# Sample attention and mLSTM in one block: heads between the key and value steps, a zeroed score bank, the sample rows of x read a second time

## The chip, the core and the metric

The kernel runs on one core of a Trainium2 chip. The metric is the device time of one execution in microseconds (us), median of several runs. A core has engines with a queue of instructions each: TensorE (PE; its weight loads are listed as PEld), VectorE (DVE), ScalarE (ACT), and SyncE (SP), which here issues most transfers. An engine takes its instructions in order and waits at semaphores. Matmul results go to the accumulator memory PSUM, which the kernel uses in banks of 512 columns.

## What is computed

One step of a decoder layer for a prompt of 256 tokens and for 8 samples of 4 tokens (32 rows). A normalised input goes through one projection that feeds two branches, an mLSTM with a matrix memory and a windowed attention; both are projected, gated and added, and a mixture of 32 experts follows. The change touches the two branches. From the reference, cut:

```python
# attention of a sample, per group (window, dilation): keys gathered from the cache and the new tokens
kg, vg = kf[:, idx], vf[:, idx]
s = einsum('bthe,btjhe->bthj', q, kg) * (E ** -0.5)
p, l, lse = masked_softmax_stats(s, valid)
o = einsum('bthj,btjhe->bthe', p, vg) / l[..., None]
...
# mLSTM, per chunk and head
b = cumsum(fc);  dmat = where(causal, b_j - b_s + ic_s, -inf);  mj = maximum(b + m, max(dmat))
sc  = (q k^T) * exp(dmat - mj);   a_int = exp(b + m - mj)
num = sc @ v + a_int * (C q);     den = sum(sc) + a_int * (n q)
h   = num / maximum(abs(den), exp(-mj))
C_new = a_c * C + sum_s ws_s v_s k_s^T;   n_new = a_c * n + sum_s ws_s k_s
...
h = h * sigmoid(o);  h = h * rsqrt(mean(h*h) + EPS) * norm_w        # per head
u = sigmoid(ga) * (hA @ w_pa) + sigmoid(gb) * (hB @ w_pb)
```

## The kernel before

The program is a row of blocks; all engines meet at the end of a block. The blocks are: the input projection, the prompt's attention, **the sample attention** (block at line 748), **the mLSTM** (block at line 957), the projection of both branches with the router (line 1309), the experts (line 1853) and the end. The order inside a block is written out by hand, one function for each engine.

*Sample attention.* The keys and values of the caches come in 16 loads of 1792 KB (KT_cache, then VK, line 757) through four slots KV: kv0, kv1 and two parts of za. Load i waits until step i-4 has been used (s_used). TensorE transposes the new queries and keys, makes the new scores, and takes eight key steps (line 777), which sum masked queries (qmask, which VectorE makes) times keys in psA. VectorE masks the scores and takes their maximum (lines 885 and 889), ScalarE takes exp (814), VectorE normalises (892), TensorE transposes the probabilities (784), ScalarE copies them out (818), and eight value steps follow (794). Then VectorE picks out each row's own sample (own, hBs), and TensorE turns the result for hBT. Beside the key steps VectorE also does the mLSTM's gate arithmetic on rows of 4 partitions: lf, prefix sums and maxima by doubling, and six pieces of xrow (877, 880).

*mLSTM.* Columns of cg, emj and ws are made from the rows by small products (1001 to 1005) and copied to colsb. For each of the four heads of the prompt: transposed q and k (994, copied out by ScalarE at 1095 and VectorE at 1141), scores (1013, 1015) with the row maxima (1017), exponent arguments (1152 to 1154), exp (1100), weights wt (1159), the state product (1026, 1029) of keys weighted by VectorE (wk, 1145), which ScalarE copies out for C_p and n_p, and the output products (1034 to 1036), which VectorE divides and gates (finish, 1132 to 1135). The next head's transposes are issued ahead of a head's state product. After the heads come the samples: scores, weights, and the products on eight state tiles of 1 MB (CT, 1070), which SP loads from the block's start into parts of za, xT, h and a tile of its own. As tiles in za are used, w_pa is loaded over them in four pieces (973). VectorE normalises the heads, and the transposed result hAT (1063, 1079, 1207, 1220) feeds the next block, whose first product is line 1298.

## Time and profile before

| | |
|---|---|
| median of 3 runs | 1636.36 us (1634.91 to 1640.58) |
| the profiled execution | 1636.94 us |
| its span, first to last instruction | 1635.2 us |
| mean granted TensorE clock | 0.965 |
| TensorE, VectorE, ScalarE busy | 1488.8, 650.2, 216.8 us |
| transfers | 584.17 MB, 357 GB/s over the span |
| sample attention, first product to the next block's | 365.53 to 445.35 us |
| mLSTM, likewise | 445.35 to 511.90 us |

The profile is of one execution, and its times count from the span's start. An engine's busy time is that in which it executes an instruction; waits are not counted. "PEclk" is the granted share of TensorE's full clock, 1.00 for 2.4 GHz and 0.50 for 1.2 GHz. "DMA share" is the mean busy share of the core's 16 transfer engines. An fp32 matmul leaves two records, so "x24" are twelve matmuls. In a list in order of time the brackets at a row's end give the engine's idle time before it and what released it.

### The profile page before, as it was taken

The numbers are of one execution on the slowest core, as the hardware profiler recorded it, in microseconds if no ns is written. First come the engines' busy times: TensorE is split into PE (matmuls) and PEld (weight loads), VectorE is DVE, ScalarE is ACT, GpSimd is POOL, SyncE is SP. The second block draws the span as 40 slices with busy tenths as digits, with TensorE's granted clock in tenths as the row PEclk, the third lists the DMA queues.
The fourth block names the chain that finished last, engine by engine and source line by source line (L and its number), as shares of the span: only waits on it lengthen the run. The fifth ranks groups of instructions, "written<-read, shape, count | busy, mean of one in ns | idle before, by whom it ended". The sixth has DMA issues, their size and how long they took to land. (4 is left out here: it accounts for less than half of the span.)

```text
span 1635.2 us, 20121 instructions
## 1 busy us (share of the span) xinstructions
PE 1488.8 (91%) x8061; PEld 710.5 (43%) x8061; DVE 650.2 (40%) x1050; ACT 216.8 (13%) x390; POOL 0.3 (0%) x5
## 2 busy tenths in 40 slices
PE   6999999864686998999999999999999999999977
PEld 4777776651553444333333333333333333333333
DVE  5555565345043614233333324333333333323343
ACT  2101110221030002011111101111011111101122
POOL 0000000000000000000000000000000000000000
PEclk9999999987787998999999999999999999999988
DMA  5888889499667992899999999999999999999960
GB/s 185 312 333 312 308 324 365 185 311 426 258 221 273 378 408 103 338 396 428 428 429 428 428 429 428 429 429 428 428 428 429 429 428 427 429 429 429 428 254 29
DMA packets 70528, 584.17 MB, mean 357 GB/s; under 512 B 6060, under 2 KB 8592, under 8 KB 42704
## 3 DMA queue, kind: packets, MB, share of 16 engines
q1 hardware_dynamic: 63856, 572.07, 85.7%
q10 hardware_dynamic: 6624, 11.41, 1.9%
q8 instruction: 37, 0.61, 0.1%
q14 instruction: 11, 0.09, 0.0%
HBM read 569.78 MB, written 67.80 MB: 390 GB/s over the span
## 5 line engine op out<-in xcount | busy, mean ns | idle before, releaser
L1676 PE MATMUL eG<-ring,hBT 128*64 128x512 f32 x1008 | 262.6, 599 | 2.3 <-DMA ring<-w 2.3
L1676 PE MATMUL eL<-ring,hBT 128*64 128x512 f32 x1008 | 259.0, 592 | 0.0
L1718 PE MATMUL eY<-ring,hBT 128*64 128x512 f32 x1024 | 233.9, 598 | 22.0 <-ACT hBT L1758 22.0
L1827 DVE SCALAR_TENSOR_TENSOR h<-eS,rgg,h 128x512 f32<-128x512 f32 (+1 forms) x192 | 135.0, 743 | 208.9 <-PE eS L1702 205.1
L1800 DVE TENSOR_SCALAR xT<-eG 128x512 f32<-128x512 f32 x32 | 22.1, 692 | 301.9 <-PE eL L1676 301.9
L411 PE MATMUL psT<-whi,xhi 128*128 128x512 f32 x336 | 136.6, 407 | 2.8 <-ACT zg L485 2.8
L1676 PEld LDWEIGHTS eL<-ring,hBT 128*64 128x64 f32 x1008 | 72.4, 137 | 143.9 <-issue 143.9
L411 PE MATMUL psT<-wlo,xhi 128*128 128x512 f32 x336 | 132.2, 393 | 0.0
L411 PE MATMUL psT<-whi,xlo 128*128 128x512 f32 x336 | 131.5, 391 | 0.0
L1718 PEld LDWEIGHTS eY<-ring,hBT 128*64 128x64 f32 x1024 | 68.0, 136 | 144.5 <-issue 114.9
L1676 PEld LDWEIGHTS eG<-ring,hBT 128*64 128x64 f32 x1008 | 66.1, 136 | 129.5 <-issue 120.1
L352 DVE CAST whi<-wraw 128x2048 fp32r<-128x2048 f32 x41 | 50.3, 1228 | 121.6 <-PE psT L415 121.4
L353 DVE TENSOR_TENSOR wlo<-wraw,whi 128x2048 fp32r<-128x2048 f32 x42 | 96.3, 2292 | 1.4
L1652 PE MATMUL eA<-zg,selU 128*64 128x512 f32 x396 | 92.3, 602 | 1.7 <-DVE selU L1789 1.7
L1767 ACT ACTIVATE xT<-xT 128x512 f32<-128x512 f32 x32 | 20.2, 631 | 467.6 <-DVE xT L1800 467.6
L411 PEld LDWEIGHTS psT<-whi,xhi 128*128 128x128 f32 x336 | 63.4, 189 | 29.0 <-issue 16.4
L1702 PE MATMUL eS<-yS,selT 128*128 128x512 f32 x192 | 71.8, 455 | 3.4 <-DVE yS L1813 2.7
L411 PEld LDWEIGHTS psT<-whi,xlo 128*128 128x128 f32 x336 | 63.4, 189 | 14.1
L411 PEld LDWEIGHTS psT<-wlo,xhi 128*128 128x128 f32 x336 | 63.5, 189 | 11.9
L1298 PE MATMUL pX<-za,xT 128*128 128x512 f32 x128 | 62.3, 640 | 2.3 <-PEq L957 2.3
L1702 PEld LDWEIGHTS eS<-yS,selT 128*128 128x128 f32 x192 | 29.1, 190 | 81.2 <-issue 75.5
L1652 PEld LDWEIGHTS eA<-zg,selU 128*64 128x64 f32 x396 | 28.7, 139 | 59.4 <-issue 57.2
(416 smaller groups left out, 1265.3 us busy)
## 6 DMA issues: line engine op xcount, KB each, us to landing
ring<-w SPq DMA_DIRECT2D x190, 2048.0 KB, 18.6
wraw<-w_in SPq DMA_DIRECT2D x42, 1024.0 KB, 7.1
k_s<-cache_k SPq DMA_DIRECT2D x8, 2040.0 KB, 10.7
v_s<-cache_v SPq DMA_DIRECT2D x8, 2040.0 KB, 31.6
ring<-CT ACTq DMA_DIRECT2D x8, 1024.0 KB, 19.4
C_s<-ring SPq DMA_DIRECT2D x8, 1024.0 KB, 10.6
k_s<-cache_k SPq DMA_DIRECT2D x4, 2032.0 KB, 9.8
v_s<-cache_v SPq DMA_DIRECT2D x4, 2032.0 KB, 9.7
```

What stands on the lines that cost most here:

```text
L352: return (lambda: dve.tensor_copy(high, raw), lambda: dve.tensor_tensor(low, raw, high.bitcast(F32), ALU.subtract))
L353: lambda: dve.tensor_tensor(low, raw, high.bitcast(F32), ALU.subtract))
L411: last = pe.matmul(ps[:, c, :], a[:, k0 + k, t * P:(t + 1) * P], b[:, k, c * 512:(c + 1) * 512], start=(k0 + k == 0 and a is xh and b is w ...
L1298: last = pe.matmul(pX[t][:, c, :], xt[:, k, t * P:(t + 1) * P], wts[k][:, c * 512:(c + 1) * 512], start=(k == 0), stop=(k == kt - 1))
L1652: last = pe.matmul(pA[64 * c:64 * c + 64, :], selU[:, t, 0:CAP], x2[:, t, c * 512:(c + 1) * 512], start=(t == 0), stop=(t == 2))
L1676: last = pe.matmul(ps[64 * hh:64 * hh + 64, :], xgT[:, k % 4, (k // 4) * CAP:(k // 4 + 1) * CAP], src[:, c, col:col + 512], start=False, s ...
L1702: pe.matmul(pSc[c][:, :], selT[:, t * P:(t + 1) * P], yS[:, c, :], start=True, stop=True).then_inc(S["sc"], 1)
L1718: last = pe.matmul(pY[64 * hh:64 * hh + 64, :], acT[:, k % 4, (k // 4) * CAP:(k // 4 + 1) * CAP], ring[:, c, col:col + 512], start=False, ...
L1767: act.activation(sg, glu, ACT.Sigmoid, scale=ALPHA).then_inc(S["sg"], 1)
L1800: dve.tensor_scalar(glu, pG[:, :], LIMIT, None, ALU.min).then_inc(S["glu"], 1)
L1827: dve.scalar_tensor_tensor(out=x, in0=pSc[c][0:R, :], scalar=rgg[0:R, t:t + 1], in1=x, op0=ALU.mult, op1=ALU.add).then_inc(S["acc"], 1)
```

## The change

The two blocks become one. The mLSTM's work for the prompt's heads is cut into pieces that stand between key steps and value steps in TensorE's order; ScalarE's and VectorE's orders follow. To have room, nearly all buffers of the mLSTM move into tiles that are free by then: transposed q and k and the exponents into xT, weighted keys and outgoing states into h, the sample head's buffers into ssS, sqk and zm. Since h's third row block is overwritten too, the next block reads the sample rows of x again, and VectorE waits for that. PSUM holds psA in three banks, whose first carries two score groups and is cleared by a new memset, since only the second bank's key matmuls still begin with start; q and k transposes share one bank and are issued apart (trans_q, trans_k), row maxima share one with the columns and the n products, and denominators are products of their own in the bank of the scores. The state tiles go into cb, kv0, kv1, za and zm as these come free, in the queue behind the last cache load, and C_p and n_p are issued by ScalarE. The old block's bodies, whose commands mostly recur, are left out here.

```diff
+    xrest = xT[:, :, :].rearrange("p k n -> p (k n)")
+    qkT_ = xrest[:, 0:4 * SEQ].rearrange("p (a n) -> p a n", a=4)
+    qT_, kT_ = qkT_[:, 0:2, :], qkT_[:, 2:4, :]
+    arg, ex, wt = (xrest[:, 4 * SEQ + i * 3 * P:4 * SEQ + (i + 1) * 3 * P] for i in range(3))
...
+    qmm = zm[:, 1, 0:2, :].rearrange("p c (b n) -> p c b n", b=NB)
...
+    ct = [state_rows(x) for x in (cb[:, a0:a0 + TILE], kv0[:, 0:TILE], kv1[:, 0:TILE], zaflat[:, 0:TILE], zaflat[:, TILE:2 * TILE],
+                                  zaflat[:, 2 * TILE:3 * TILE], zaflat[:, 3 * TILE:4 * TILE],
+                                  zm[:, 0, 0:2, :].rearrange("p c n -> p (c n)"))]
...
+    psA = pb(ap, "psA", [P, 3, 512])
+    psV = psA[:, 0:2, :].rearrange("p a (b e) -> p (a b) e", e=AD)
+    psN = psA[:, 2, 3 * P:4 * P]
+    psTR = pb(ap, "mTR", [P, 512])
+    psSC = pb(ap, "mSC", [P, 512])
+    psC = pb(ap, "mC", [P, 512])
+    psN_ = pb(ap, "mN", [P, 512])
+    psMX = pb(ap, "mMX", [P, 512])
+    psM, psX = psMX[:, 0:SEQ], psMX[:, SEQ:2 * SEQ]
+    den = lambda t: psSC[:, 3 * P + t:3 * P + t + 1]
...
+    SEGS = ((0, 0, 0, 1, 0), (1, 0, 1, 4, 1), (0, P, 5, 2, 2))
...
+            sp.wait_ge(s_new, 1)
+            sp.wait_ge(s_qm, 4)
+            sp.dma_start(nrow, n_rows).then_inc(s_ld, 16)
+            sp.dma_start(ntok, n_tok).then_inc(s_ld, 16)
+            for i, (ready, value) in enumerate(((s_nm, 1), (s_used, 13), (s_used, 14), (s_used, 15), (s_used, 16), (s_used, 16),
+                                                (s_used, 16), (s_wk, 2 * MH))):
+                if i >= 4:
+                    sp.wait_ge(s_ct[i % 4], 16)
+                if i == NB - 1:
+                    sp.wait_ge(s_mtse, MH)
+                sp.wait_ge(ready, value)
+                sp.dma_start(ct[i], CT[:, :, i].rearrange("p h k v -> p h (k v)")).then_inc(s_ct[i % 4], 16)
+            for i in range(4):
+                sp.wait_ge(s_cq, 4 + i)
+                sp.dma_start(wa[:, 2 * i:2 * i + 2, :],
...
+            def columns():
+                pe.wait_ge(s_xr, 6)
...
+            def head_scores(hd):
+                pe.wait_ge(s_col, 2)
+                if hd >= 1:
+                    pe.wait_ge(s_w_, hd)
+                    pe.wait_ge(s_hh, 2 * hd)
+                    pe.wait_ge(s_co, 2 * hd)
+                pe.wait_ge(s_mte, hd + 1)
+                pe.wait_ge(s_mtse, hd + 1)
...
+            def head_out(hd):
+                pe.wait_ge(s_w_, hd + 1)
+                if hd >= 1:
+                    pe.wait_ge(s_hh, 2 * hd)
+                wts = ((0, 0, 0, True, True), (1, 1, 0, True, False), (1, 2, 1, False, True))
+                for to, w_, tk, first, end in wts:
+                    pe.matmul(psN_[:, to * MD:(to + 1) * MD], wt[:, w_ * P:(w_ + 1) * P], vaug[:, tk, hd, 0:MD], start=first, stop=end)
+                    last = pe.matmul(den(to), wt[:, w_ * P:(w_ + 1) * P], vaug[:, tk, hd, MD:MD + 1], start=first, stop=end,
+                                     skip_group_check=True)
...
+            trans_q(0)
+            pe.wait_ge(s_te, 2)
             for g in range(3):
-                last = pe.matmul(psN[:, 0:AD], spT[:, 7 + g, :], zaw[:, 6 + g, :], start=(g == 0), stop=(g == 2))
+                last = pe.matmul(psA[:, 2, g * P:(g + 1) * P], sqk[:, g, :], sqk[:, 3 + g, :], start=True, stop=True)
+            last.then_inc(s_new, 1)
+            trans_k(0)
+            pe.wait_ge(s_qm, 4)
+            for b in range(4):
+                key_scores(b)
+            columns()
+            head_scores(0)
+            key_scores(4)
+            head_state(0)
+            trans_q(1)
+            key_scores(5)
+            head_out(0)
+            trans_k(1)
+            key_scores(6)
+            head_scores(1)
+            key_scores(7)
+            head_state(1)
+            trans_q(2)
+            head_out(1)
+            trans_k(2)
+            head_scores(2)
+            pe.wait_ge(s_pr, 1)
+            for n in range(10):
+                last = pe.transpose(psA[:, n // 4, (n % 4) * P:(n % 4 + 1) * P], ssS[:, n * P:(n + 1) * P], ident)
+                if n % 4 == 3 or n == 9:
+                    last.then_inc(s_pt, 1)
+            head_state(2)
+            trans_q(3)
+            pe.wait_ge(s_pe, 3)
+            key_values(0)
+            key_values(1)
+            head_out(2)
+            trans_k(3)
+            key_values(2)
+            key_values(3)
+            head_scores(3)
+            key_values(4)
+            head_state(3)
+            key_values(5)
+            head_out(3)
+            key_values(6)
+            key_values(7)
...
+            for i in range(NB):
+                pe.wait_ge(s_ct[i % 4], 16 * (i // 4 + 1))
+                for half in range(2):
+                    for j in range(MH):
+                        last = pe.matmul(psC[32 * j:32 * j + 32, 0:MD], qmm[:, half, i, 32 * j:32 * j + 32],
+                                         ct[i][:, j, half * MD:(half + 1) * MD],
+                                         start=(i == 0 and half == 0), stop=(i == NB - 1 and half == 1))
+                last.then_inc(s_cq, 1)
...
+                act.wait_ge(s_co, 2 * hd + 2)
+                act.dma_start(C_p[hd].rearrange("(a p) e -> p a e", p=P),
+                              cst[:, hd % 2].rearrange("p (a e) -> p a e", a=2)).then_inc(s_cst[hd % 2], 16)
+                act.dma_start(n_p[hd:hd + 1], nst[:, hd % 2]).then_inc(s_cst[hd % 2], 16)
...
+            head_exp(0)
+            state_out(0)
+            evac_q(1)
+            squares(0)
+            head_exp(1)
+            state_out(1)
+            evac_q(2)
             act.wait_ge(s_nm, 1)
             act.activation(ssS[:, :], ssS[:, :], ACT.Exp, bias=sst[:, 0:1], accum_out=sst[:, 1:2]).then_inc(s_ex, 1)
+            squares(1)
...
+            dve.memset(psA[:, 0, 0:3 * P], 0.0).then_inc(s_qm, 1)
...
+            head_keys(0)
+            dve.wait_ge(s_colp, 1)
+            dve.tensor_copy(colsb[:, 0:60], psX[:, 0:60]).then_inc(s_col, 1)
+            dve.tensor_copy(ACC, psX[0:NS, 60:61]).then_inc(s_col, 1)
+            dve.wait_ge(s_col, 2)
+            head_weighted(0)
+            head_weights(0)
+            head_weighted(1)
+            head_keys(1)
+            head_finish(0)
+            head_weights(1)
+            dve.wait_ge(s_new, 1)
+            dve.wait_ge(s_used, NB)
+            sm = CBc("smask")
+            parts = [dve.scalar_tensor_tensor(out=ssS[:, a:a + n], in0=psA[:, bank, at:at + n], scalar=SCALE, in1=sm[:, a:a + n],
+                                              op0=ALU.mult, op1=ALU.add)
+                     for bank, at, a, n in ((0, 0, 0, P), (1, 0, P, 4 * P), (0, P, 5 * P, 2 * P), (2, 0, NKEY, 3 * P))]
+            link.many(*parts)
+            dve.tensor_reduce(sst[:, 0:1], ssS[:, :], AX.X, ALU.max, negate=True).then_inc(s_nm, 1)
+            head_weighted(2)
+            head_keys(2)
+            head_finish(1)
+            dve.wait_ge(s_ex, 1)
+            link(dve.reciprocal(sst[:, 2:3], sst[:, 1:2]))
+            dve.tensor_scalar(ssS[:, :], ssS[:, :], sst[:, 2:3], None, ALU.mult).then_inc(s_pr, 1)
+            head_weights(2)
+            head_weighted(3)
+            head_keys(3)
+            head_finish(2)
+            head_weights(3)
+            head_finish(3)
...
+            sp.dma_start(h[0:NS, 2, :], x_sample.rearrange("b t d -> (b t) d")).then_inc(s_hload, 16)
...
-            dve.wait_ge(s_hload, 80)
+            dve.wait_ge(s_hload, 96)```

How the queues change is shown at three places. First TensorE behind key step 3. Before, the next key step stood there (line 777, three shapes of products for each):

```order
L777 MATMUL psA<-kv,qmask 32x128 [waits s_kv0]
L777 MATMUL psA<-kv,qmask 32x128 x3
L777 MATMUL psA<-kv,qmask 32x512 x4
L777 MATMUL psA<-kv,qmask 32x256 x4
L777 MATMUL psA<-kv,qmask 32x128 [waits s_kv1]
```

Now (854 to 858 the columns, 869 to 873 a head's scores and row maxima, 904 a key step, 882 and 885 a state product):

```order
L854 MATMUL mMX<-ca,cg 128x4 [waits s_xrow]
...
L869 MATMUL mSC<-xT 128x256 [waits s_mtk_out,s_mtq_out,s_cols]
L869 MATMUL mSC<-xT 128x256
L871 MATMUL mSC<-xT 128x128 x2
L873 MATMUL mMX<-mx,cb 128x256
L904 MATMUL psA<-kv,qmask 32x128 [waits s_kv0]
L904 MATMUL psA<-kv,qmask 32x128 x3
L904 MATMUL psA<-kv,qmask 32x512 x4
L904 MATMUL psA<-kv,qmask 32x256 x4
L882 MATMUL mC<-h,vaug 128x256 [waits s_arg,s_wk]
L882 MATMUL mC<-h,vaug 128x256 x3
```

Key step 4 now stands behind a wait for xrow and behind head 0's scores, and pieces of a head stand between the later steps too.

Second VectorE around the mask and the maximum of the sample scores. Before:

```order
L885 SCALAR_TENSOR_TENSOR ssS<-psA,cb 128x128 [waits s_kv_used,s_newscores]
L885 SCALAR_TENSOR_TENSOR ssS<-psA,cb 128x512
L885 SCALAR_TENSOR_TENSOR ssS<-psA,cb 128x256
L885 SCALAR_TENSOR_TENSOR ssS<-psA,cb 128x384
L889 TENSOR_REDUCE sst<-ssS 128x1 [waits s_steps]
L891 RECIPROCAL sst<-sst 128x1 [waits s_sexp]
L892 TENSOR_SCALAR ssS<-ssS,sst 128x1280 [waits s_steps]
```

Now (1210 and 1214 mask and maximum, 1176 weighted keys, 1170 the copy of transposed keys, 1161 to 1164 a finish, 1219 and 1220 the normalisation):

```order
L1189 SCALAR_TENSOR_TENSOR xT<-mSC,xT 128x384 [waits s_num,s_mscores,s_mexp]
L1210 SCALAR_TENSOR_TENSOR ssS<-psA,cb 128x128 [waits s_kv_used,s_newscores]
...
L1214 TENSOR_REDUCE sst<-ssS 128x1 [waits s_steps]
L1176 TENSOR_SCALAR h<-zm,colsb 128x256 [waits s_cprod]
L1176 TENSOR_SCALAR h<-zm,colsb 128x256
L1170 COPY xT<-mTR 128x512 [waits s_mscores,s_mtrans2]
L1161 TENSOR_SCALAR sm<-mSC 128x1 [waits s_num]
...
L1164 SCALAR_TENSOR_TENSOR zm<-mN,sm,zm 128x256 [waits s_steps]
L1219 RECIPROCAL sst<-sst 128x1 [waits s_sexp]
L1220 TENSOR_SCALAR ssS<-ssS,sst 128x1280 [waits s_steps]
```

Two heads' work now stands ahead of the mask, and head 1's keys and finish stand between the maximum and the normalisation.

Third SP's queue of state tiles and w_pa. Before, at the start of the mLSTM's block:

```order
L966 DMA za<-CT 128x4x512 [waits s_stored]
L966 DMA za<-CT 128x4x512 x3
L966 DMA xT<-CT 128x4x512 [waits s_ct0]
L966 DMA ct<-CT 128x4x512 [waits s_ct1]
L966 DMA ct<-CT 128x4x512 [waits s_ct2]
L966 DMA h<-CT 128x4x512 [waits s_ct3]
```

Now, behind the last cache load:

```order
L806 DMA za<-VK 128x3584 [waits s_kv_used] x2
L809 DMA sqk<-n_rows 32x256 [waits s_qmask,s_newscores]
L810 DMA sqk<-n_tok 128x256
L818 DMA cb<-CT 128x4x512 [waits s_snegmax]
L818 DMA kv<-CT 128x4x512 [waits s_kv_used] x2
L818 DMA za<-CT 128x4x512 [waits s_kv_used]
L818 DMA za<-CT 128x4x512 [waits s_kv_used,s_ct0]
L818 DMA za<-CT 128x4x512 [waits s_kv_used,s_ct1]
L818 DMA za<-CT 128x4x512 [waits s_kv_used,s_ct2]
L818 DMA zm<-CT 128x4x512 [waits s_wk,s_mtk_out,s_ct3]
L821 DMA za<-w_pa 128x2x1024 [waits s_cq] x4
L256 DMA n_s<-sqk 32x256 [waits s_nnew_out]
```

The first four tiles were issued at once; now all but the first wait for a value step, and the last four for an earlier tile too.

## Rows read from the trace of the kernel before

**Rows 1.** Stretches: busy us (count) by engine, granted clock, DMA share, GB/s

```profile
core 0: us, PE busy (x) PEld busy (x) DVE busy (x) ACT busy (x) POOL busy (x), PEclk, DMA share, GB/s
437.00:446.00 9.00, 5.03 (x68) 4.19 (x69) 3.68 (x4) 0.00 (x0) 0.00 (x0) 0.80 0.00 2
472.00:497.00 25.00, 19.00 (x102) 11.99 (x104) 14.34 (x48) 8.99 (x25) 0.00 (x0) 0.86 0.07 26
643.00:1587.00 944.00, 909.70 (x4112) 324.65 (x4113) 329.97 (x547) 110.15 (x195) 0.00 (x0) 0.99 0.98 413
```

**Rows 2.** In order of time, TensorE: key steps 4 and 5 (start, length)

```profile
387.47 3.22 PE L777 MATMUL psA<-kv,qmask 128*32 128x128 f32 x24 [2.14 <-DMA kv<-KT_cache]
391.76 1.72 PE L777 MATMUL psA<-kv,qmask 128*32 128x128 f32 x24 [1.08 <-DMA kv<-KT_cache]
```

**Rows 3.** In order of time, VectorE: the last xrow piece, a key copy

```profile
388.64 0.19 DVE L880 TENSOR_TENSOR xrow<-aint,cb 4x32 f32<-4x32 f32 x1
...
457.34 0.68 DVE L1141 COPY mqkT<-mTR 128x512 f32<-128x512 f32 x1
```

**Rows 4.** Stretches of VectorE: mask and maximum; one head's finish

```profile
402.60:406.00 3.40, 3.17 (x5) 0.50 0.97 413
462.50:464.80 2.30, 1.95 (x8) 1.00 1.05 404
```

**Rows 5.** Stretches inside the mLSTM, columns as in rows 1

```profile
446.00:460.00 14.00, 12.82 (x50) 10.27 (x49) 3.33 (x10) 1.40 (x3) 0.00 (x0) 0.52 0.93 310
460.00:485.00 25.00, 22.47 (x106) 15.09 (x106) 12.61 (x44) 8.34 (x24) 0.00 (x0) 1.00 0.53 202
485.00:490.00 5.00, 2.16 (x13) 1.72 (x13) 3.15 (x13) 3.13 (x11) 0.00 (x0) 1.00 0.15 53
490.00:495.00 5.00, 3.12 (x19) 1.54 (x20) 3.34 (x9) 1.89 (x3) 0.00 (x0) 0.52 0.00 0
450.00:470.00 20.00, 18.71 (x72) 13.21 (x72) 8.34 (x27) 4.29 (x12) 0.00 (x0) 0.76 1.04 383
```

**Rows 6.** In order of time, TensorE: columns and head 0

```profile
446.82 0.37 PE L1001 MATMUL mX<-ca,cg 4*128 4x4 f32 x2
...
451.17 2.05 PE L1013 MATMUL mSC<-mqkT 128*128 128x256 f32 x4 [1.18 <-DVE mqkT L1141]
...
455.14 1.97 PE L994 MATMUL mTR<-ca,zm 128*128 128x128 f32 x8
456.90 3.15 PE L1026 MATMUL mSC<-wk,vaug 128*128 128x256 f32 x8
...
460.94 0.70 PE L1034 MATMUL mN<-vaug,wt 128*128 128x257 f32 x2
```

**Rows 7.** In order of time, TensorE: head 1

```profile
462.62 1.10 PE L1013 MATMUL mSC<-mqkT 128*128 128x256 f32 x4
...
464.72 1.10 PE L994 MATMUL mTR<-ca,zm 128*128 128x128 f32 x8
465.66 1.89 PE L1026 MATMUL mSC<-wk,vaug 128*128 128x256 f32 x8
...
468.44 0.70 PE L1034 MATMUL mN<-vaug,wt 128*128 128x257 f32 x2
...
469.41 0.60 PE L1036 MATMUL mN<-vaug,wt 128*128 128x257 f32 x2
```

**Rows 8.** In order of time: SP issues load 12, TensorE takes value step 4

```profile
416.61 2.87 SPq L757 DMA_DIRECT2D kv<-VK  x2
...
424.08 1.74 PE L794 MATMUL psV<-kv,qmask 128*32 128x128 f32 x56 [1.94 <-DMA kv<-VK]
```

**Rows 9.** In order of time, TensorE and VectorE: the block's end

```profile
503.96 1.29 DVE L1207 TENSOR_TENSOR xT<-mTR,cols 128x512 f32<-128x512 f32 x2 [1.50 <-PE mTR L1063]
504.28 1.07 PE L1070 MATMUL mN<-h,qmm 128*32 128x256 f32 x16
...
509.50 0.49 DVE L1220 TENSOR_TENSOR xT<-mTR,cols 128x128 f32<-128x128 f32 x2 [0.42 <-PE mTR L1079]
...
511.90 8.15 PE L1298 MATMUL pX<-za,xT 128*128 128x512 f32 x12 [2.33 <-PEq L957]
```

501 lines of the change are left out of this document (211 added, 290 removed).

## The prediction

> **What bounds the kernel now.** I read the stretches of time first, then the lists of instructions in order of time inside the stretch that the change touches. One execution spans 1635.2 us. From 643 to 1587 the expert stage runs at a granted clock of 0.99 with its transfers at a share of 0.98 [rows 1]; the change moves no instruction there, so whatever it gains or loses is made between 365 and 512 and shifts the rest as a block. In that window no resource binds all the time. In the sample attention the transfers set the pace: a key step takes TensorE 3.22 us at the low clock and 1.72 at the high one, but its steps start 4.29 us apart and wait for a load [rows 2], 1.8 MB each. Then come two stretches almost without transfers: 437 to 446 moves 2 GB/s and 472 to 497 moves 26 GB/s [rows 1]. In the first the sample attention finishes and its block ends; in the second the state tiles have landed and the heads are still being computed, in a chain through TensorE, VectorE and ScalarE of which none is full (19.0, 14.3 and 9.0 of 25 us). So loads with little arithmetic are followed by arithmetic without loads, until the next block's first product at 511.90 [rows 9].
>
> **The sum.** No large operation disappears. The merged block issues the same 15 cache loads, 8 state tiles and 4 w_pa pieces, and nearly the same matmuls. What it can remove is waiting. I follow it in three legs, in TensorE's new order, with the prices of the old rows.
>
> *Leg 1, to the end of the row arithmetic.* TensorE takes key steps 0 to 3 as before, then stands at columns() for xrow, whose last piece VectorE starts at 388.64 and ends 0.19 later [rows 3]. VectorE's queue is the same up to there but for one new memset of a 128x384 score bank. No row shows a memset; it lies between nothing and the 0.68 of a 128x512 copy [rows 3], and I take 0.5, nearer to the copy. Leg 1 ends at 389.4. Key 4 had arrived at 387.47 [rows 2] and waits now: a stall that the change makes, some 4 us of TensorE after key 3.
>
> *Leg 2, to the end of value step 0.* Here TensorE sets the pace, and its clock the price. After its last pause the old block ran at 0.52 from 446 to 460 and at 1.00 from 460 to 485 [rows 5]. I price the pieces right after the new stall by the low rows: the columns and their copy-out, 446.82 to 451.17, are 4.35 us; a head's scores, to 455.14, 3.97; a state product, 456.90 to 460.94, 4.04 [rows 6]; a key step 3.22 [rows 2]. That is 15.6 us, to 405.0. From there I take the high rows [rows 7]: scores 462.62 to 464.72 are 2.1, eight transposes to 465.66 are 0.94 (0.47 for each half, as the halves now stand apart), a state product to 468.44 is 2.78, the output products to 470.0 are 1.6. These are now six matmuls in place of three, with a one-column product for each denominator. No row shows the three new ones; they lie between nothing and another 1.6, and I take 0.4, nearer to nothing, for one column is little against 256. Up to the end of value step 0 remain five transpose halves (2.35), three key steps (5.16), two outputs (4.0), two scores (4.2), two state products (5.56), ten probability transposes (1.2) and the step itself (1.74 [rows 8]): 24.2 us. Two waits come on top. Head 1's scores wait until VectorE has finished head 0, since the denominators share their bank: a key copy and a head finish, 0.68 and 2.1 [rows 3, 4], against one transpose half and a key step on TensorE, so about 1 us. Head 2's scores wait longer: after key 7 VectorE masks and reduces the sample scores (3.2), weights and copies keys (about 1.3, twice the copy) and finishes head 1 (2.1) [rows 3, 4], partly after the state product and the transposes that these need, some 8.6 us, while TensorE has 5.8: 2.8 us. Leg 2 ends at 405.0 + 24.2 + 3.8 = 433.0. With the low prices throughout, the 24.2 are about 40 and the end is 449; with the high ones from the start it is 426.
>
> In this leg the transfers are *not* the limit. Key 7 ends near 416, load 11, which takes its slot, has landed by about 423, and load 12 must wait for value step 0. The transfers idle for some 10 us; there a part of the gain is given back.
>
> *Leg 3, the transfers after value step 0.* From here SP's queue has work without a break: loads 12 to 15, each released by a value step; eight state tiles, released by values 3 to 7 and by the tiles before them; w_pa, released by the products on the tiles. The old load 12 went out at 416.61 and value step 4 started on it at 424.08: 7.5 us [rows 8]. Three more at 4.29 make 453.4. A state tile is 1.05 MB; at the 383 GB/s of 450 to 470 [rows 5] it takes 2.74 us, and eight tiles and four pieces of w_pa of the same size take 32.9: 486.3. Behind them SP waits for the store of n_s. No row shows that wait; it is between nothing and one more tile's 2.74, and I take 1. From the last VectorE instruction to the next block's product the rows have 509.99 to 511.90 [rows 9], 1.9. That gives 489.2 against 511.9: **22.7 us**.
>
> The engines must keep up with that, and they just do. Values 1 to 7 with what stands between them are 7 x 1.74 + 2.1 + 2.78 + 4.0 + 0.47, so value 7 ends at 455, right after its load. A tile's product is 1.07 [rows 9], so the products end with the last tile at 475.3 if they start by 467, twelve us after value 7, which leaves room for the sample head's scores. The old tail from the last product, 505.35 to 509.99 [rows 9], is 4.6; the four copies of hA at 0.65 [rows 9] and the waits between them now follow it too, 4 us. That ends near 485, within 2 us of SP's end. Moving C_p and n_p to ScalarE's queue puts eight issues there, beside an engine that was busy 9.0 of 25 us [rows 1]; uncovered they would cost a few tenths each. The second read of the sample rows is 128 KB in a queue whose result is not wanted for another 100 us: nothing, or 0.3 at the same 383 GB/s if it were.
>
> The sum is made against the profiled execution, 1636.94 us, which is 0.6 above the median of 1636.36. With 22.4 off the median I predict **1614.0**.
>
> **A rule that speaks against it.** The rows show both sides of the clock: 0.52 from 490 to 495, after five us in which TensorE was busy 2.16, and 1.00 for the 25 us in which it was busy 22.5 [rows 5]. The merged order keeps it as busy as the latter, hence the high prices after 405. The Trainium skill, "TensorE: Matmul & The Clock Gate", section "A second HAM failure mode: psum-queue depth-cycling", says that frequent short idles between groups of matmuls can keep the clock going back and forth and cost throughput, and the new order has a wait at nearly every piece. The trace shows such swings, but only after waits for a load; by that rule the time would be rival B's.
>
> **The rivals.**
>
> *A, the forecast* (high clock from about 405, transfers set the end): 1609 to 1621, chance 0.60.
>
> *B, the clock goes back and forth through the block.* Then a piece costs about halfway between its two prices: the 24.2 us become 32, value step 0 ends at 441, and TensorE instead of the transfers sets the pace after it, with about 5 more in the values and 3 to 8 in the sample head and the tail. The block ends between 495 and 502 and the time is 1621 to 1629. For it: 0.52 lasted for 14 us in which TensorE was busy 12.8 [rows 5]. Against: it then held at 1.00 on the very same pieces. 0.20.
>
> *C, better than the forecast:* no low stretch after the stall at xrow. Value step 0 ends at 426 and all behind it moves along: 1603 to 1609. Against it stands the same row from 446 to 460. 0.08.
>
> *D, slower: TensorE at the low level from the stall to the end.* Leg 2 ends at 449, the values with head 3 take 41 more, the sample head, the state products and the copies 28: the block ends near 518 and the next starts at 520, 8 us late, 1644. It decides against the change once more than about eight tenths of the block's TensorE work is at the low level. Against it: 1.00 over 25 us. 0.06.
>
> *E, no change:* the waits for VectorE in leg 2 and the sample tail are each several us longer than worked out, and the idle transfers of [rows 1] come back elsewhere. It would take 17 us or more of such waits: 1632 to 1641. 0.06.
>
> **How the numbers follow.** A measurement of this kernel tells about 0.3%, 4.9 us, from no change. The likeliest case gives 1614.0; the range runs from about the middle of C, 1605, to the top of B, 1629, and leaves D, E and half of C outside. A, B and C are faster by more than that: 0.88; E is the same, 0.06; D is slower, 0.06.
>
> **What would show it.** In the new profile TensorE should stand some 4 us for xrow after key step 3; the clock should be near 0.5 for about 15 us after that and near 1.0 then; value step 0 should start near 431, the transfers be nearly idle for 8 to 10 us before it and near a share of 1 from it to about 486; the first product of the next block should start near 489, and the stretch from there to the end be as long as now, 1123 us. If value step 0 starts at 440 or later, leg 2 is wrong, by clock or by a wait for VectorE; if the transfers have gaps after it, the engines and not SP set the end.

## The result, and the profile after

The changed kernel takes **1616.4 us** (median of 4 runs, 1611.3 to 1617.0), the kernel before 1637.5 on the same chip: ratio 0.986, 95% interval 0.984 to 0.989. Predicted were 1614.0, in a range of 1605 to 1629, and faster with a chance of 0.88. The difference is 21 us; predicted were 22.4.

The profiled execution took 1617.02 us (span 1615.2), 19.9 less than that of before. I split it by two issues of SP, the first load of the merged block (m_rows) and the first of the next block (wb). Before, they are 365.48 and 511.85, after 363.50 and 488.96. So the program reaches the block 2.0 us earlier, the block takes 125.5 us in place of 146.4 (**-20.9**), and from the next block to the end it is 1126.2 in place of 1123.4 (**+2.9**). Predicted were -22.7, and 1123 for the rest. The 2.0 us are scatter: the change touches nothing ahead of the block, and in the 14 profiles of this document it begins anywhere between 363.0 and 368.2.

The clock and the transfers in stretches of the new block, read as [rows 1] and [rows 5] were:

```profile
core 0: us, PE busy (x) PEld busy (x) DVE busy (x) ACT busy (x) POOL busy (x), PEclk, DMA share, GB/s
390.00:400.00 10.00, 9.63 (x44) 5.81 (x45) 2.13 (x8) 0.80 (x2) 0.00 (x0) 0.55 0.68 265
400.00:420.00 20.00, 17.62 (x141) 10.81 (x139) 8.96 (x25) 6.05 (x14) 0.00 (x0) 1.00 0.95 370
420.00:430.00 10.00, 8.03 (x28) 6.50 (x28) 3.79 (x13) 3.17 (x9) 0.00 (x0) 0.66 0.08 29
430.00:434.00 4.00, 4.00 (x90) 2.83 (x92) 0.61 (x2) 1.45 (x3) 0.00 (x0) 1.00 0.18 66
434.00:485.00 51.00, 39.15 (x593) 27.65 (x583) 21.02 (x60) 6.89 (x19) 0.00 (x0) 0.86 1.01 392
```

Two stretches without transfers have become one, 420 to 434, and behind it the transfers run at a share of 1.01 for 51 us. TensorE in order of time, the rows behind a wait, value step 0 (the row x112 is steps 0 and 1), the last product on a state tile, and the next block's first weight load and product:

```profile
380.33 1.72 PE L904 MATMUL psA<-za,qmask 128*32 128x128 f32 x24 [2.58 <-DMA za<-KT_cache]
387.22 0.37 PE L854 MATMUL mMX<-ca,cg 4*128 4x4 f32 x2 [5.17 <-DVE xrow L1156]
...
394.76 3.22 PE L904 MATMUL psA<-kv,qmask 128*32 128x128 f32 x24
...
409.18 1.10 PE L869 MATMUL mSC<-xT 128*128 128x256 f32 x4 [1.35 <-issue]
...
421.98 1.11 PE L869 MATMUL mSC<-xT 128*128 128x256 f32 x4 [3.00 <-issue]
422.91 1.02 PE L871 MATMUL mSC<-xT 128*128 128x128 f32 x4
423.87 1.22 PE L873 MATMUL mMX<-mx,cb 4*128 4x256 f32 x2
425.02 2.40 PE L952 MATMUL psA<-ca,ssS 128*128 128x128 f32 x10
...
431.84 3.27 PE L915 MATMUL psA<-kv,qmask 128*32 128x128 f32 x112
...
478.16 1.94 PE L998 MATMUL mC<-zm 128*32 128x256 f32 x16 [0.76 <-DMA zm<-CT]
...
488.98 0.50 PEld L1367 LDWEIGHTS pX<-za,xT 128*128 128x128 f32 x2 [2.16 <-DMA za<-w_pa]
489.01 8.17 PE L1367 MATMUL pX<-za,xT 128*128 128x512 f32 x12 [1.79 <-PEq L797]
```

The wait for xrow is there (key steps 3 and 4 are rows 1 and 3), and so are the waits ahead of the scores of heads 1 and 2. The brackets name "issue" there, so the releaser has to be found in VectorE's list; it is the finish of the head before, whose last piece ends 0.21 us ahead of head 2's scores:

```profile
421.29 0.48 DVE L1164 SCALAR_TENSOR_TENSOR zm<-mN,sm,zm 128x256 f32<-128x256 f32 x1
421.69 0.15 DVE L1219 RECIPROCAL sst<-sst 128x1 f32<-128x1 f32 x1
421.87 0.89 DVE L1220 TENSOR_SCALAR ssS<-ssS,sst 128x1280 f32<-128x1280 f32 x1
...
480.24 0.48 DVE L1270 TENSOR_SCALAR sqk<-mC,colsb 128x256 f32<-128x256 f32 x1 [11.22 <-PE mC L998]
...
487.04 0.51 DVE L1288 TENSOR_TENSOR xT<-psA,cols 128x128 f32<-128x128 f32 x2 [0.57 <-PE psA L1016]
```

SP's queue, from the release of load 12 by value step 0 to the next block:

```profile
433.64 2.05 SPq L806 DMA_DIRECT2D kv<-VK  x2
...
467.35 0.54 SPq L818 DMA_DIRECT2D zm<-CT  x1
469.26 8.58 SPq L821 DMA_DIRECT2D za<-w_pa  x4
477.88 0.46 SPq L256 DMA_DIRECT2D n_s<-sqk  x1
...
488.96 0.41 SPq L1382 DMA_DIRECT2D wb<-w_pb  x1
```

### The profile page after: what moved, and what is told of

Its sections match the earlier page's. It is cut to its first block and busy times, and to the rows that moved or that the text cites. A ratio compares the mean times of both kernels' runs of the same rounds, so it can differ in the third digit from the quotient of the medians.

```text
span 1615.2 us, 20168 instructions
## 1 busy us (share of the span) xinstructions
PE 1486.9 (92%) x8085; PEld 711.4 (44%) x8085; DVE 650.2 (40%) x1051; ACT 217.4 (13%) x390; POOL 0.3 (0%) x5
## 5 line engine op out<-in xcount | busy, mean ns | idle before, releaser
L1367 PE MATMUL pX<-za,xT 128*128 128x512 f32 x128 | 62.0, 638 | 1.8 <-PEq L797 1.8
L1722 PEld LDWEIGHTS eA<-zg,selU 128*64 128x64 f32 x396 | 28.4, 137 | 58.1 <-issue 56.0
```

The lines of the kernel that those rows point to most:

```text
L1367: last = pe.matmul(pX[t][:, c, :], xt[:, k, t * P:(t + 1) * P], wts[k][:, c * 512:(c + 1) * 512], start=(k == 0), stop=(k == kt - 1))
L1722: last = pe.matmul(pA[64 * c:64 * c + 64, :], selU[:, t, 0:CAP], x2[:, t, c * 512:(c + 1) * 512], start=(t == 0), stop=(t == 2))
```

## The experiments

Runs of one kernel differ by up to 12 us here (the kernel before, 1628.6 to 1640.4 on one chip), so beside each ratio, which is to the kernel before on the same chip, I read from the profile the block's length (m_rows to wb, as above) and the starts, counted from m_rows, of head 1's and head 2's scores and of value step 0. "Rest" is from wb to the span's end.

There is one profile of each run, and the block's length has a scatter of its own. In the interleaved runs the columns start 23.7 us after m_rows (24.2 in e2). From there to head 0's scores it takes 3.5 us where they run at the low clock and down to 2.2 where they run at the high one, and the level differs between runs whose edits come later (3.5 in e3, 2.3 in e6). So differences of up to 1.3 us between blocks can be scatter.

| run | head 1, head 2 | value 0 | block | rest | median us | ratio to before |
|---|---|---|---|---|---|---|
| before | | | 146.4 | 1123.4 | 1637.5 | 1 |
| changed | 45.7, 58.5 | 68.3 | 125.5 | 1126.2 | 1616.4 | 0.986 (0.984 to 0.989) |
| e1 sequential | 85.4, 99.0 | | 149.6 | 1125.9 | 1647.0 | 1.007 (1.005 to 1.010) |
| e2 key 4 first | 46.0, 60.3 | 71.4 | 128.5 | 1126.5 | 1618.9 | 0.988 (0.986 to 0.991) |
| e3 softmax first | 45.4, 63.8 | 59.1 | 121.5 | 1124.0 | 1615.5 | 0.988 (0.986 to 0.990) |
| e4 wait filled | 45.0, 57.8 | 64.4 | 121.4 | 1124.3 | 1614.6 | 0.987 (0.985 to 0.990) |
| e5 other bank | 43.6, 54.7 | 62.1 | 119.3 | 1129.3 | 1616.0 | 0.987 (0.984 to 0.990) |
| e6 softmax, values first | 45.0, 64.9 | 58.7 | 120.6 | 1125.3 | 1616.9 | 0.987 (0.984 to 0.990) |
| e7 early tail | 45.7, 58.5 | 68.4 | 126.4 | 1126.1 | 1619.2 | 0.988 (0.985 to 0.991) |
| e8 late second read | 45.0, 57.8 | 67.6 | 124.6 | 1123.9 | 1613.0 | 0.984 (0.981 to 0.987) |
| e9 combined | 43.6, 64.6 | 58.1 | 115.7 | 1125.9 | 1608.3 | 0.983 (0.981 to 0.986) |
| e10 changed again | 45.8, 58.6 | 68.4 | 125.2 | 1127.5 | 1618.2 | 0.989 (0.986 to 0.991) |
| e11 sequential, other bank | 84.5, 94.4 | | 140.7 | 1128.7 | 1636.9 | 1.001 (0.999 to 1.003) |
| e12 e5, code longer | 43.6, 54.7 | 62.1 | 119.1 | 1125.5 | 1611.1 | 0.984 (0.982 to 0.987) |

**e1: the halves one after the other.** TensorE's order; those of VectorE and ScalarE follow it.

```diff
-            for b in range(4):
+            for b in range(NB):
                 key_scores(b)
...
             pe.wait_ge(s_pr, 1)
...
             pe.wait_ge(s_pe, 3)
+            for b in range(NB):
+                key_values(b)
+            columns()
+            for hd in range(MH):
+                head_scores(hd)
+                head_state(hd)
+                if hd < 3:
+                    trans_q(hd + 1)
+                head_out(hd)
+                if hd < 3:
+                    trans_k(hd + 1)
```

> One block as in the changed kernel, but the two halves one after the other: all key steps, the sample softmax, all value steps, then columns() and the four heads; the sample head and the state tiles as they are. What it tells apart: is the gain made by running the heads between the key and value steps (theory 1), or already by having one block in place of two, with its state tiles requested earlier (rival 2)? Theory 1: in the trace before, the last sample product is issued at 440.5 and columns() starts at 446.8, and only those 6 us and a block change can be saved; the heads and the transfers stand behind one another again, and the block is 5 to 10 us shorter than before, 11 to 16 longer than in the changed kernel: 1626 to 1632 us, ratio 0.994 to 0.997. Rival 2: nearly the whole gain stays, 1614 to 1619 us.

It is slower than before, which neither theory expected. The scores of heads 1 to 3 in its TensorE list:

```profile
449.48 2.04 PE L869 MATMUL mSC<-xT 128*128 128x256 f32 x4 [3.00 <-issue]
...
463.11 2.04 PE L869 MATMUL mSC<-xT 128*128 128x256 f32 x4 [3.00 <-issue]
...
476.74 2.01 PE L869 MATMUL mSC<-xT 128*128 128x256 f32 x4 [3.01 <-issue]
```

A head takes 13.63 us, against 11.45 for head 0 before (451.17 to 462.62, [rows 6, 7]), part of it at the low clock, and 8.51 and 8.65 for heads 1 and 2 (to 471.13 and 479.78). There is a wait of 3.0 in each and the low clock behind it (2.04 for what takes 1.10 at the high one). So rival 2 falls: as the changed kernel is made, merging by itself costs 3.2 us of block, and the interleaving covers that cost too.

**e2: key step 4 in the wait for xrow.**

```diff
-            for b in range(4):
+            for b in range(5):
                 key_scores(b)
             columns()
             head_scores(0)
-            key_scores(4)
+            key_scores(5)
             head_state(0)
             trans_q(1)
-            key_scores(5)
+            key_scores(6)
             head_out(0)
             trans_k(1)
-            key_scores(6)
             head_scores(1)
```

> TensorE takes key step 4 ahead of columns(), in the pause of 5.17 us that the changed kernel has there, and each later key step moves up one place (5 to head 0's state, 6 to its output, 7 ahead of head 1's scores where 6 was; nothing else). Theory 1 (TensorE's leg up to value step 0 gates the transfers, and everything behind moves with value step 0): the leg loses a key step of 1.7 to 3.2 us, value step 0 starts at 428 to 430 in place of 431.8, the next block 2 to 3.5 us earlier: 1613 to 1614 us. Rival 1 (the engines' tail, not the leg, sets the end): value step 0 moves, but the end stays within 1 us: 1616. Rival 3 (the clock): the pause left is 3.4 us, and if TensorE's clock doesn't fall in it the pieces up to 400 go at the high price, worth another 5 us: value step 0 at 424, 1609.

All three are refuted. TensorE has a key step less to do ahead of head 1, and head 1's scores start at 46.0, as in the changed kernel (45.7): they wait 3.00 us in place of 1.35. What sets their start isn't TensorE's work but the round trip of head 0: scores, weights, output products, finish. The longer wait is followed by scores at the low clock, and value step 0 comes 3.1 us later.

**e3: the sample softmax and value steps 0 and 1 ahead of head 2.**

```diff
 # VectorE
-            head_keys(2)
-            head_finish(1)
             dve.wait_ge(s_ex, 1)
...
+            head_keys(2)
+            head_finish(1)
 # TensorE
-            head_scores(2)
             pe.wait_ge(s_pr, 1)
...
+            pe.wait_ge(s_pe, 3)
+            key_values(0)
+            key_values(1)
+            head_scores(2)
             head_state(2)
             trans_q(3)
-            pe.wait_ge(s_pe, 3)
-            key_values(0)
-            key_values(1)
             head_out(2)
```

> The sample softmax goes ahead of head 2: VectorE normalises before it copies head 2's keys and finishes head 1, ScalarE copies the transposed probabilities before head 1's squares, and TensorE does the ten transposes and value steps 0 and 1 before head 2's scores. In the changed kernel the exponentials' maximum is ready at 416.7, the transposes start at 425.0, value step 0 at 431.8, and the transfers idle from about 420 to 434. Theory 1: value step 0 starts at 421 to 424, load 12 goes out some 8 to 10 us earlier, the idle stretch of the transfers nearly closes; the engines then lose a part, since heads 2 and 3 move back: the next block starts 5 to 8 us earlier, 1608 to 1612 us. Rival 1: heads 2 and 3 and the tail take what value step 0 gains, the end moves by at most 2 us, 1614 to 1616.

Value step 0 comes 9.3 us earlier, as theory 1 wanted, and the block gains 3.9, less than it wanted. The time, 1615.5, is in rival 1's range. Loads 14 and 15 went out at 74.5 after m_rows, against 75.9 in the changed kernel, since value steps 2 and 3 still stood behind head 2.

**e4: TensorE kept busy in the wait for xrow.**

```diff
+            for _ in range(34):
+                pe.transpose(psC[:, 0:P], ident, ident)
             columns()
```

> 34 transposes of the identity into a bank that is not yet in use, right behind key step 3: about 4 us of needless work of TensorE in the pause of 5.17 us before columns(). It removes no wait, it only keeps the engine busy. Rival 3 (the clock falls because of that pause, and the low pieces from 387 to 400 are what the pause costs beside itself): the granted clock stays near 1.0, the pieces from columns() to head 0's state product, 387.2 to 401.3 in the changed kernel, take 9 us in place of 14.1, value step 0 starts 4 to 5 us earlier and the time is 1611 to 1612 us. Theory 1 with a clock that falls for another reason: no change, or up to 1 us longer where the transposes outlast the wait, 1616 to 1617.

```profile
core 0: us, PE busy (x) PEld busy (x) DVE busy (x) ACT busy (x) POOL busy (x), PEclk, DMA share, GB/s
384.00:390.00 6.00, 4.63 (x45) 4.39 (x43) 4.48 (x20) 0.90 (x3) 0.00 (x0) 1.00 1.00 425
390.00:402.00 12.00, 11.64 (x53) 7.09 (x53) 2.13 (x8) 0.80 (x2) 0.00 (x0) 0.57 0.84 336
402.00:430.00 28.00, 23.64 (x181) 15.51 (x183) 13.37 (x39) 9.78 (x25) 0.00 (x0) 1.00 0.69 254
```

The first low stretch came all the same, behind the columns instead of ahead of them, so rival 3's cause is wrong. The block is still 4.1 us shorter, for two other reasons. The columns now run mostly at the high clock, and from their start to head 0's scores it is 2.2 us in place of 3.5. And the second low stretch, 420 to 430 in the changed kernel, is gone, although the wait of 3.00 us ahead of head 2's scores is the same: from these scores to value step 0 it is 6.6 us in place of 9.9. Value step 0 moved by 3.9, the block by 4.1: with the leg's order unchanged, the end follows value step 0 one for one.

**e5: the denominators in another bank.** In the scores' bank they make the next scores wait for the finish.

```diff
-    den = lambda t: psSC[:, 3 * P + t:3 * P + t + 1]
+    den = lambda t: psA[:, 2, 3 * P + t:3 * P + t + 1]
 # head_scores
-                    pe.wait_ge(s_hh, 2 * hd)
 # head_out, hd >= 1
+                    pe.wait_ge(s_nm, 1)
 # ahead of the new values' product into psN
+            pe.wait_ge(s_hh, 2 * MH)
```

> The two denominator columns of a head move from the bank of its scores to a free part of the third bank of the sample scores. Nobody writes there between a head's output products and its finish, so a head's scores no longer wait until VectorE has finished the head before (the wait of 1.35 us ahead of head 1's scores and most of the 3.00 us ahead of head 2's). Theory 1a, formed from the runs so far: up to value step 0 not TensorE's own work but the round trip scores, weights, output products, finish, next scores sets the pace, because the denominators share the scores' bank. Then head 1's scores start 1.3 us earlier and head 2's 2 to 3 (they still wait for the keys that VectorE copies after the sample maximum), the second low stretch of the clock (420 to 430) shortens or goes, value step 0 starts at 64 to 66 us after the block's first load in place of 68.3, and the block is 3 to 5 us shorter: 1611 to 1613. Rival: VectorE's own work (mask, maximum, key copies) is as late as the finish; head 2's scores gain less than 1 us and the time is 1615 to 1616.

Theory 1a holds, and the gain is larger than it expected: head 1's scores 2.1 us earlier, head 2's 3.8, value step 0 6.2, the block 6.1. Not all of it is the edit's. Of the 6.2 us, 0.9 stand ahead of head 0's scores (the columns), 2.9 are the shorter way from there to head 2's scores, and 2.4 the way on to value step 0, where the clock stays at 1.00 (from 402 to 445); e4 shows that the second low stretch can go without this edit. Head 2's scores still wait 0.87 us, for the keys that VectorE copies. The time didn't move, since the block starts 2.0 us later in the program and the rest is 3.1 longer. In the last block of the program TensorE starts 2.9 us after the other engines:

```profile
420.10 1.10 PE L868 MATMUL mSC<-xT 128*128 128x256 f32 x4 [0.87 <-DVE xT L1171]
...
1563.31 0.34 SPq L1972 DMA_DIRECT2D ring<-norm_f  x1
1563.33 1.06 ACT L2019 ACTIVATE zg<-h 32x1024 f32<-32x1024 f32 x1 [10.16 <-PEq L1924]
...
1566.19 2.99 PE L1988 MATMUL fT<-ca,h 32*128 32x32 f32 x16 [7.15 <-issue]
```

**e6: value steps 2 and 3 ahead of head 2 as well.** To the edit of e3 this is added.

```diff
-            key_values(0)
-            key_values(1)
+            for b in range(4):
+                key_values(b)
             head_scores(2)
...
-            key_values(2)
-            key_values(3)
             head_scores(3)
```

> As the run with the softmax ahead of head 2, with value steps 2 and 3 also ahead of head 2's scores (there they stood behind its output and released loads 14 and 15 only at 74.5 us after the block's first load). Theory 1 (the release of the transfers by the first value steps sets the end): loads 12 to 15 go out at 62 to 66, the transfers never idle after the first of them, the last state tile lands at about 106 in place of 111 and the block takes 118 to 120 us in place of 121.5, against 125.5 in the changed kernel: 1609 to 1611. Rival 1 (the engines): heads 2 and 3 move back by four value steps, so value step 7 and the sample head end later than the tiles land; the products on the tiles no longer wait for transfers, and the block stays at 121 to 124 us: 1612 to 1615.

Between the two: loads 14 and 15 went out at 63.6, 11 us earlier than in e3, and the block is 0.9 shorter than there, no more than the columns' clock accounts for (2.3 us against 3.5). Head 3's scores wait 3.00 us for head 2's finish, value step 4 stands behind them, and it releases the second state tile, issued at 82.2 (in e3 at 79.8). The wait removed at one head had become a wait at another.

**e7: the rows' transposes ahead of the products on the state tiles.** The sixteen transposes, that of hBs and their copies move ahead of the products and of the sample head's finish; TensorE's part:

```diff
+            pe.wait_ge(s_hb, 1)
+            pe.transpose(psA[:, 2, 0:P], hBs[:, :], ident).then_inc(s_t, 1)
+            pe.wait_ge(s_ha, 8)
...
             pe.wait_ge(s_qmm, 3)
             for i in range(NB):
...
-            pe.wait_ge(s_hb, 1)
-            pe.transpose(psA[:, 2, 0:P], hBs[:, :], ident).then_inc(s_t, 1)
-            pe.wait_ge(s_ha, 8)
```

> The transposes of the normalised prompt rows and of hBs, with their copies by VectorE, go ahead of the products on the state tiles; behind the last product stay the sample head's finish, its norm and its two transposes. Work and transfers are the same. In the changed kernel VectorE ends 7.3 us after the last product starts its wait, and w_pa's transfers end at about the same time. Theory 1 (the transfer queue sets the end, as predicted): the tail shortens by about 3 us, but w_pa's last piece still lands when it did: the block gains 0 to 1 us, 1615 to 1616. Rival 1 (the engines' tail sets the end): 2.5 to 3.5 us, 1613 to 1614.

```profile
485.61 0.49 DVE L1287 TENSOR_TENSOR xT<-psA,cols 128x128 f32<-128x128 f32 x2 [0.42 <-PE psA L1016]
491.39 0.41 SPq L1381 DMA_DIRECT2D wb<-w_pb  x1
...
491.40 0.50 PEld L1366 LDWEIGHTS pX<-za,xT 128*128 128x128 f32 x2 [5.96 <-DMA za<-w_pa]
```

VectorE is done 5.3 us before the next block, which now waits for w_pa. The block is 1.0 us longer, which neither theory expected. The moved work delayed the products on the first tiles by 8 us; these release w_pa, whose first piece goes out 7.3 us later after m_rows, and the transfers, which have no gap there in the changed kernel, fall to a share of 0.52 from 478 to 480. So this run doesn't separate the tail from the transfers; e9 does.

**e8: the second read of the sample rows behind the state stores.**

```diff
-            sp.dma_start(h[0:NS, 2, :], x_sample.rearrange("b t d -> (b t) d")).then_inc(s_hload, 16)
             sp.dma_start(wr[:, :, :], w_router).then_inc(s_sm, 16)
...
                 sp.dma_start(C_s[:, :, b].rearrange("p h k v -> p h (k v)"), ctile[b]).then_inc(s_cts, 16)
+            sp.dma_start(h[0:NS, 2, :], x_sample.rearrange("b t d -> (b t) d")).then_inc(s_hload, 16)
```

> The second read of the sample rows of x moves on SP's queue from ahead of the small loads of the next block to behind the stores of the sample states; it is needed only some 50 us later. It tells what that read costs. In the traces with it the next block reaches the products on hBT 57.7 to 58.0 us after its first load (56.3 in one), in the one before without it 54.9. If the read, between the loads of the states that ScalarE issues, delays those states, the stretch goes back to about 55 and the time to 1613 to 1614. If it costs what its 128 KB take (0.3 us), as predicted, the stretch stays at 57.7 and the time at 1616; the 3 us are then an accident of how loads and stores of the states share the transfer engines.

The products on hBT start 55.5 us into the next block (543.29), in place of 57.9 in the changed kernel (546.81) and 57.4 in e10; before it was 54.9. In e9, which has this edit too, they start at 55.7; in the runs without it, between 56.3 and 58.0, in the mean 57.3. So where it stands the read costs between 0.6 and 2.5 us, some 1.7 in the mean, not 0.3. The block's 0.9 us are within its scatter.

**e9: combined.** The edits of e6 and e8; the other bank for heads 0 and 2 alone; value step 4 behind head 2's state, 5 and 6 one place earlier; a group of the rows' transposes behind each of the products on tiles 3 to 6. **e10** is the changed kernel beside it. Of e9's edit what isn't shown above:

```diff
-    den = lambda t: psSC[:, 3 * P + t:3 * P + t + 1]
+    den = lambda hd, t: (psA[:, 2, 3 * P + t:3 * P + t + 1], psSC[:, 3 * P + t:3 * P + t + 1])[hd % 2]
 # TensorE
             head_state(2)
+            key_values(4)
             trans_q(3)
...
                 last.then_inc(s_cq, 1)
+                if 3 <= i < 7:
+                    rows_half(i - 3)
```

> What the runs so far point to, together: the denominators of heads 0 and 2 in the third bank of the sample scores (head 1's and head 3's scores no longer wait for a finish), the sample softmax and value steps 0 to 3 ahead of head 2, value step 4 behind head 2's state, the rows' transposes woven between the products on the state tiles (one behind each of products 3 to 6, so that they fill waits for tiles and hold nothing up), and the second read of the sample rows behind the state stores. Theory 1a (round trip of the heads up to value step 0, from there the transfers): value step 0 at 56 to 57 us after the block's first load, the transfers without a break from 60, the last piece of w_pa at about 114, the block 114 to 117 us in place of 125.5, and the stretch up to the products on hBT 2 us shorter: 1604 to 1608. Rival 1 (the engines): the products on the tiles start only at 100 or later, because heads 2 and 3 moved back, and the block stays at 119 to 121: 1609 to 1613.

> The changed kernel once more, unedited, beside the combined version, so that both are timed on one chip: 1615 to 1618 us, with a block of 125 to 126 us. If its profile differs by more than 1 us in the stretch up to the next block's products on hBT (57.85 before), that stretch isn't tied to the order of the small loads.

```profile
421.08 3.54 PE L916 MATMUL psA<-kv,qmask 128*32 128x128 f32 x112 [0.54 <-ACT qmask L1078]
...
468.00 1.07 PE L1007 MATMUL mC<-zm 128*32 128x256 f32 x16
...
473.35 0.51 DVE L1291 TENSOR_TENSOR xT<-psA,cols 128x128 f32<-128x128 f32 x2 [0.56 <-PE psA L1020]
478.74 0.41 SPq L1385 DMA_DIRECT2D wb<-w_pb  x1
```

9.7 us less block than the changed kernel, 9.5 less than e10, and 9.9 us less time than e10 on the same chip; the block is as theory 1a had it, the time 0.3 above its range. VectorE is done 4.9 us before the next block, which waits for w_pa, and from 430 to 475 the transfers run at a share of 0.98 to 1.06: behind value step 0 they alone set the end. In e10 the block is again 125.2, while its rest is 1.2 us longer than in the first profile of the same kernel.

**e11: the halves in sequence, with e5's edit.**

> The run with the two halves one after the other, with the denominators moved to the third bank of the sample scores as in the run that did this alone. In the sequential run the heads' scores started 13.63 us apart with a wait of 3.0 us for the finish in each, and the block took 149.6 us, 3.2 more than the two blocks before. Theory 1a: without that wait the heads are about 11.5 us apart, as the old ones were (451.17 to 462.62), the block takes 142 to 144 us, 2 to 4 less than before, and the time is 1632 to 1637; what is left to the changed kernel's 125.5 is the interleaving. Rival 2 (the merge itself pays): below 136 us.

The heads are 9.9 us apart and the block 140.7, shorter than theory 1a expected, but above the 136 of rival 2. With the bank no longer shared, merging by itself does save 5.7 us of block against the two blocks before, though the time is the same. Against the same version interleaved, e5, it is 21.3 us longer; with the shared bank (e1 against the changed kernel) 24.1. TensorE's late start in the last block, 3.1 us, is in this run too.

**e12: e5 with 16 idle transposes behind key step 3,** as e4 has 34.

> The run with the denominators in another bank, with 16 transposes of the identity into an idle bank behind key step 3, where TensorE stands 5 us for xrow: they cost no time there, but they lengthen TensorE's program ahead of everything that follows. What it tells apart: that run's block was 6.1 us shorter than the changed kernel's, its time not; in the last block of the program TensorE's first transposes started at 1566.19, 2.9 us after ScalarE's first instruction, with nothing that the trace shows to wait for, and so they did in the sequential run with the same edit (1586.79, 3.1 us) and in no other run (0.04 to 0.06). If it is the position in TensorE's program (its code being fetched there), the lengthened program doesn't meet it: TensorE starts there within 0.1 us of the others, the rest after the block takes 1126 in place of 1129 us, and the time is 1611 to 1614. If it hangs on the edit itself (the other bank, the waits), the 2.9 us stay and the time is 1615 to 1617. In both cases the block is 118 to 120 us.

```profile
1561.27 1.06 ACT L2021 ACTIVATE zg<-h 32x1024 f32<-32x1024 f32 x1 [9.37 <-PEq L1926]
1561.29 2.96 PE L1990 MATMUL fT<-ca,h 32*128 32x32 f32 x16 [3.82 <-PEq L1926]
```

The block is as short as in e5, and the late start is gone: 1611.1 us. So the edit by itself doesn't bring it. That it hangs on where the code stands in TensorE's program fits, on one profile of each.

## Why the prediction was right

**The mechanism and the total.** The gain was to come from overlap alone, given back in part while the transfers idle ahead of value step 0, and it did. Sequential against interleaved is 21 to 24 us (e1, e11), and the block's change is -20.9. Value step 0 and the block's end move together (e2, e4, e5), and e9 shows the transfers as the limit behind it. How near the total came is in part luck: the 2.0 us ahead of the block are scatter and hide most of the 2.9 lost behind it, and the second measurement, e10, is 18.3 us below the kernel before on its chip, in place of 21.

**Leg 1** held: the wait for xrow is 5.17 us where "some 4" was predicted, and key step 4 stood behind it.

**Leg 2** came out right for a partly wrong reason. Counted from m_rows its end was to be at 67.5 (433.0 less 365.48) and was near 70.1 (load 12 goes out at 433.64); the transfers idled for some 12 us ahead of it, in place of 8 to 10. The waits ahead of heads 1 and 2, 1.0 and 2.8, measured 1.35 and 3.00. The step that failed is "here TensorE sets the pace, and its clock the price". The sum of TensorE's pieces gave nearly the right end only because the waits had been added to it; with less TensorE work ahead of head 1 the end doesn't move forward (e2), without the shared bank it moves by 6.2 us (e5), 2.9 of them between head 0's and head 2's scores. Up to head 2 the bound of this leg is each head's round trip through VectorE, and behind it the clock adds 3.3 us. The clock was low for 12 us in place of 15, and then, unpredicted, once more from 420 to 430: ten transposes 2.40 in place of the 1.2 of the sum, a state product 4.05 in place of 2.78. From head 2's scores to value step 0 it is 9.9 us, against 6.6 at the high clock (e4). That is a part of rival B: low stretches came again near 465 and from 474 on, where the transfers set the pace. The prediction's remark that the old trace shows such swings only after waits for a load is wrong for one of its own stretches: the 0.52 from 490 to 495 stands behind a wait for ScalarE.

```profile
489.60 0.74 PE L1045 MATMUL mSC<-sT 128*128 128x128 f32 x4 [2.84 <-ACT sT L1111]
```

**A rule that fits.** Where a bank is shared, the wait isn't a matter of the kernel's taste. The Trainium skill, "PSUM — Partial Sum Buffer", section "PSUM bank collisions raise a hardware error", has two engines kept apart by bank and quadrant of 32 partitions, in the simple version by bank, and not by address. No run here shows a collision; what the runs show is the price of keeping apart, waits of 1.35 and 3.00 us of which e5 leaves 0.87.

**Leg 3** held to a microsecond: from the end of value step 0 to the next block's product it was to be 56.2 us (433.0 to 489.2) and was 55.4 from load 12's issue (433.64 to 489.01), at 392 GB/s where 383 was assumed. The products on the tiles ended at 480.1 in place of 475.3, and VectorE's tail at 487.55 in place of 485, within the 2 us of SP's end that were claimed. The tail was at the low clock again. In the changed kernel the next block's first weights wait for w_pa until 488.98, 1.4 us after VectorE's end, and in e9, with the engines done 4.9 us earlier than the next block, they still do: the transfers are the bound there.

**The rest** was mis-sized by 2.9 us, all of it ahead of the products on hBT (54.9 us into the next block before, 57.9 now; from there to the end 1068.4 in both). The term is "nothing, or 0.3" for the second read of the sample rows. It costs 0.6 to 2.5 us (e8, e9) where it stands, ahead of the router's weights and biases while ScalarE's state loads are under way. It is not shown what of its issue or its packets delays the states.

**Between block and time.** e5 and e11 show that a gain in a block can be lost far behind it: 2.9 and 3.1 us at the program's end. Even in the other profiles the unchanged code from the products on hBT to the end takes 1066.3 to 1070.2 us.

## What to carry to other kernels

Before adding up an engine's work, look for the round trip: if a result's bank is written again by the next step, that step waits for the reader on the other engine, and moving two columns to an idle bank took more off the block here (6.1 us, about half of it ahead of head 2's scores, where the waits stood) than any reordering by itself (at most 4.9, e6). When work is interleaved, issue first what releases the transfers, and then follow what stands behind each release, or the wait only moves on (e3 to e6). Judge a block by its own length in the profile as well as by the program's time, since places far behind it can take the gain back.

## What the hardware showed unexpectedly

*Code position.* In two runs of twelve, both with e5's edit, TensorE began the program's last block 2.9 and 3.1 us late, with no wait that the trace names; in all other profiles it was at most 0.1. With 16 more transposes far ahead of it, e5's late start was gone (e12). The Trainium skill, "Runtime: NRT & Kernel Launch", section "Instruction fetch mechanics", says that a taken branch to code outside the loaded pages has to wait for a fetch. The block ahead of this one ends in a branch over a second pass of the experts. No run here shows the fetch itself, and that it is the cause remains a conjecture.

*The clock.* It fell to the low level about the columns whether TensorE idled 5.17 us ahead of them (changed kernel: 0.60 from 385 to 387, within that wait, then 0.50) or, filled with transposes, 1.37 (e4: 1.00 up to 390, behind most of the columns, then 0.57). The same wait of 3.00 us ahead of head 2's scores was followed by the low level in the changed kernel and by the high one in e4. What decides between the two stays open; that the waits alone don't is shown.
